# Moving the routing work of two expert layers: logits and turned rows tile by tile, modulation products behind them, places ahead of the rests

## The reference

```
g_prob = softmax(x @ w_group)            # 4 groups
g_sel  = argmax(g_prob + b_group)
e_prob = softmax((x @ w_expert) of the chosen group)   # 8 experts each
top-2 of e_prob + b_expert; weights normalized, times the group's probability
y[t] = sum over its 2 experts of weight * (silu(x @ w_gate[e]) * (x @ w_up[e])) @ w_down[e]
```

## Time and profile before

| | |
|---|---|
| median of three runs | 2175.79 us (2173.64 to 2178.47) |
| span of the profiled execution | 2172.9 us |
| PE busy | 2071.2 us, 95% |
| DVE, ACT busy | 1013.0 us, 718.1 us |
| mean granted TensorE clock | 0.979 |
| transfers | 621.14 MB, mean 286 GB/s |

### The profile page before, as it was taken

How to read it: one execution, slowest core, us unless ns; L and a number is a source line. 1 busy time by engine, 2 the same in 40 slices (tenths; PEclk the granted TensorE clock), 3 DMA queues, 4 the chain that set the end, 5 groups by cost and what they waited for, 6 DMA issues and landing times.

```text
span 2172.9 us, 31110 instructions
## 1 busy us (share of the span) xinstructions
PE 2071.2 (95%) x13436; PEld 1471.4 (68%) x13436; DVE 1013.0 (47%) x1665; ACT 718.1 (33%) x1074; POOL 214.5 (10%) x186
## 2 busy tenths in 40 slices
PE   5999999999999898999999998998999999999998
PEld 3855744444444696444444446987999989999998
DVE  3534511111111565111111115888579856777983
ACT  4334211111111442011111116867555444445552
POOL 0000000000000000000000000015135300003640
PEclk9999999999999999999999999999999999999999
DMA  9688799999999558999999995453455545334652
GB/s 330 211 299 321 289 411 423 422 423 422 423 423 422 213 205 331 415 423 422 423 422 423 423 423 195 156 194 118 152 159 182 187 177 132 102 117 156 193 176 97
DMA packets 220047, 621.14 MB, mean 286 GB/s; under 512 B 20544, under 2 KB 110464, under 8 KB 170496
## 3 DMA queue, kind: packets, MB, share of 16 engines
q1 hardware_dynamic: 209760, 612.80, 73.3%
q10 hardware_dynamic: 10144, 6.27, 1.0%
HBM read 617.95 MB, written 1.08 MB: 285 GB/s over the span
## 4 chain that ended last, share of the span: by engine, by line
PE 85%; DVE 6%; DMA 4%; ACT 3%; SPq 1%; issue 1%; POOL 0%; ACTq 0%; DVEq 0%
PE bank L593 31%; PE bank L1366 19%; PE bank L1375 10%; PE bank L1385 5%; PE bank L581 3%; PE bank L1345 3%; DMA ring<-in_moe_w_up 2%; PE bank L380 2%; PE bank L627 1%; PE bank L628 1%; DVE ring_rounded L309 1%; ACT ring_rounded L303 1%; DMA ring<-in_mla_w_dq 1%; PE bank L577 1%; PE bank L633 1%; SPq L280 1%
## 5 line engine op out<-in xcount | busy, mean ns | idle before, releaser
L593 PE MATMUL bank<-normed_rounded,ring_rounded 128*128 128x256 f32 x3424 | 416.0, 283 | 6.3 <-ACT normed_rounded L689 3.4
L593 PEld LDWEIGHTS bank<-normed_rounded,ring_rounded 128*128 128x128 f32 x3424 | 411.7, 189 | 8.3 <-issue 4.3
L1366 PE MATMUL bank<-ring,arena 128*64 128x512 f32 x1760 | 389.1, 592 | 3.1 <-DVE arena L1724 2.0
L1730 DVE TENSOR_TENSOR arena<-arena,bank 64x512 f32<-64x512 f32 x64 | 43.5, 680 | 648.1 <-ACT arena L1550 648.1
L309 DVE TENSOR_TENSOR ring_rounded<-ring,ring_rounded 128x4096 fp32r<-128x4096 f32 (+2 forms) x64 | 277.9, 4344 | 104.7 <-ACT ring_rounded L303 104.3
L593 PE MATMUL bank<-arena_rounded,ring_rounded 128*128 128x256 f32 (+1 forms) x2384 | 302.6, 286 | 4.5 <-ACT arena_rounded L1990 2.3
L1366 PEld LDWEIGHTS bank<-ring,arena 128*64 128x64 f32 x1760 | 127.2, 137 | 253.1 <-issue 250.0
L593 PEld LDWEIGHTS bank<-arena_rounded,ring_rounded 128*128 128x128 f32 x2384 | 290.7, 189 | 8.9 <-ACT arena_rounded L1990 3.1
L303 ACT ACTIVATE ring_rounded<-ring 128x4096 fp32r<-128x4096 f32 (+2 forms) x64 | 220.6, 3446 | 32.9 <-DMA ring<-in_ffn_w_down 31.7
L1375 PE MATMUL bank<-ring,arena 128*64 128x512 f32 x896 | 208.0, 607 | 3.8 <-ACT arena L1557 3.8
L1550 ACT ACTIVATE arena<-bank 64x512 f32<-64x512 f32 x64 | 38.1, 596 | 428.3 <-PE bank L1366 428.3
(11 more groups left out here) (286 smaller groups left out, 2154.1 us busy)
## 6 DMA issues: line engine op xcount, KB each, us to landing
ring<-in_moe_w_down SPq DMA_DIRECT2D x112, 1024.0 KB, 17.7
ring<-in_moe_w_gate SPq DMA_DIRECT2D x110, 1024.0 KB, 14.5
ring<-in_moe_w_up SPq DMA_DIRECT2D x110, 1024.0 KB, 16.2
ring<-in_w_mod SPq DMA_DIRECT2D x24, 2048.0 KB, 12.2
ring<-in_ffn_w_up SPq DMA_DIRECT2D x44, 1024.0 KB, 6.8
ring<-in_ssm_w_in SPq DMA_DIRECT2D x12, 2048.0 KB, 8.3
ring<-in_ffn_w_down SPq DMA_DIRECT2D x10, 2048.0 KB, 8.0
normed<-in_moe_w_gate SPq DMA_DIRECT2D x18, 1024.0 KB, 15.5
```

The lines of the kernel that those rows point to most:

```text
L593: end = e.matmul(out, lhs.bitcast(F32R), rhs.bitcast(F32R), start=start and n == 0 and k == 0, stop=stop and n == 2 and k == n_k - 1)
L1366: ends[i] = e.matmul(bank[rows, :], xt[:, n * KD // 2 + j, :], weights[:, j, :], start=n == 0 and j == 0, stop=n == 1 and j == KD // 2 - 1)
L1730: e.tensor_tensor(h, h, banks.of(key, "h", x)[0:cap, :], ALU.mult).then_inc(*dve.up(key, "h", x))
```

## The change

It reorders the routing of both layers. It leaves every product as it is.

- TensorE: the products with w_mod chunks 10 and 11 move from ahead of the logits to behind the turned rows. Logits and turned rows go by feature tile: for each i two logit products and two transposes. The four `row` banks are claimed ahead of these, the `acc` banks ahead of `ranks`.
- ScalarE: a first Exp of one column before the shift, so that the table is loaded there; `row high` of half 0 for both token tiles ahead of the Exp of the logits, half 1 behind it, then the modulation rows; then the eviction of `xt` parts 0 and 1, which VectorE did.
- VectorE: all four `lower` move behind `places_of(0)`, the modulation's reductions and the sum of loads; it evicts `xt` parts 2 and 3 in a row, then does weights, tables, shares 0 and 1 and `places_of(1)`; in the loop `turned_back(0)` comes behind `gated(0)`.

```diff
     def tensor(self, e, w):
-        for at in (10, 11):
-            self.last_steps.step_tensor(e, w, at, turn=False)
         k.meet(w, self.before)
...
-        for t in range(NT):
-            for i in range(KD):
-                w.wait_ge(*act.at(key, "x", i))
+        for half in range(2):
+            for t in range(NT):
+                _, emptied = banks.next(dve, key, "row", t, half)
+                w.wait_ge(*emptied)
+        for i in range(KD):
+            w.wait_ge(*act.at(key, "x", i))
+            for t in range(NT):
                 end = e.matmul(bank[:, t * n_log:(t + 1) * n_log], k.A[:, i, t * P:(t + 1) * P], self.W[:, i, :],
-                               start=i == 0, stop=i == KD - 1)
-        end.then_inc(*pe.up(key, "logits"))
-
-        for t in range(NT):
-            for half in range(2):
-                bank, emptied = banks.next(dve, key, "row", t, half)
-                w.wait_ge(*emptied)
-                for j in range(4):
-                    end = k.turn(e, bank[:, j * P:(j + 1) * P], k.A[:, 4 * half + j, t * P:(t + 1) * P])
-                end.then_inc(*pe.up(key, "row", t, half))
+                               start=i == 0 and t == 0, stop=i == KD - 1 and t == NT - 1)
+            if i == KD - 1:
+                end.then_inc(*pe.up(key, "logits"))
+            for t in range(NT):
+                at = i % 4 * P
+                end = k.turn(e, banks.of(key, "row", t, i // 4)[:, at:at + P], k.A[:, i, t * P:(t + 1) * P])
+                if i % 4 == 3:
+                    end.then_inc(*pe.up(key, "row", t, i // 4))
+        for at in (10, 11):
+            self.last_steps.step_tensor(e, w, at, turn=False)
         self.last_steps.turn_tensor(e, w, 10)
         self.last_steps.close_tensor(e, w)
...
-        first_rows, acc_emptied = [banks.next(dve, key, "xt", 0, 0)], []
...
+        first_rows = [banks.next(act if part < 2 else dve, key, "xt", 0, part) for part in range(KD // 2)]
...
-                w.wait_ge(*dve.at(key, "xt", x // TEAM, 2 * n + 1))
+                w.wait_ge(*(act if x < TEAM and n == 0 else dve).at(key, "xt", x // TEAM, 2 * n + 1))
...
     def scalar(self, e, w):
+        e.activation(k.root_of_one[:, 7:8], k.mat("ones")[:, 0:1], ACT.Exp).then_inc(*act.up())
...
+        row_high(0, 0)
+        row_high(1, 0)
+        w.wait_ge(*dve.at(key, "shifted"))
+        e.activation(self.prob, self.prob, ACT.Exp).then_inc(*act.up(key, "exp"))
+        row_high(0, 1)
+        row_high(1, 1)
         for at in (10, 11):
             self.last_steps.step_scalar(e, w, at)
...
+        for part in range(2):
+            w.wait_ge(*pe.at(key, "xt", 0, part))
+            e.activation(k_flat(self.xt[0][:, 2 * part:2 * part + 2, :]), banks.of(key, "xt", 0, part)[:, :], ACT.Copy
+                         ).then_inc(*act.up(key, "xt", 0, part))
...
     def vector(self, e, w):
-        lower(0, 0)
-        lower(0, 1)
         bank = banks.of(key, "ranks")
...
         places_of(0)
-        lower(1, 0)
-        lower(1, 1)
+        for at in (10, 11):
+            self.last_steps.step_vector(e, w, at)
         e.tensor_reduce(self.loads, ...)
+        for half in range(2):
+            for t in range(NT):
+                lower(t, half)
...
-        for part, between in enumerate((weights, shared, tables, lambda: self.last_steps.close_vector(e, w))):
-            turned_x(0, part)
-            between()
+        turned_x(0, 2)
+        turned_x(0, 3)
+        weights()
+        shared()
+        tables()
...
         shares(0)
+        shares(1)
+        places_of(1)
+        self.last_steps.close_vector(e, w)
...
-        shares(1)
-        turned_back(0)
-        places_of(1)
         for x in range(EXPERTS):
             gated(x)
+            if x == 0:
+                turned_back(0)
```

More of the change, by code:

```diff
@@ L1398, in tensor @@
         w.wait_ge(*self.router.at("router"))
-        for t in range(NT):
-            for i in range(KD):
-                w.wait_ge(*act.at(key, "x", i))
-                end = e.matmul(bank[:, t * n_log:(t + 1) * n_log], k.A[:, i, t * P:(t + 1) * P], self.W[:, i, :],
-                               start=i == 0, stop=i == KD - 1)
-        end.then_inc(*pe.up(key, "logits"))
-        for t in range(NT):
-            for half in range(2):
-                bank, emptied = banks.next(dve, key, "row", t, half)
-                w.wait_ge(*emptied)
-                for j in range(4):
-                    end = k.turn(e, bank[:, j * P:(j + 1) * P], k.A[:, 4 * half + j, t * P:(t + 1) * P])
-                end.then_inc(*pe.up(key, "row", t, half))
+        for half in range(2):
[5 more added lines that the diff above has]
+            for t in range(NT):
+                end = e.matmul(bank[:, t * n_log:(t + 1) * n_log], k.A[:, i, t * P:(t + 1) * P], self.W[:, i, :],
+                               start=i == 0 and t == 0, stop=i == KD - 1 and t == NT - 1)
[8 more added lines that the diff above has]
+            self.last_steps.step_tensor(e, w, at, turn=False)
         self.last_steps.turn_tensor(e, w, 10)
         self.last_steps.close_tensor(e, w)
+        acc_emptied = []
+        for b in range(KD // 2):
+            _, emptied = banks.next(dve, key, "acc", b)
+            banks.hold(key, "acc", b)
+            acc_emptied.append(emptied)
         bank, emptied = banks.next(dve, key, "ranks")
@@ L1535, in scalar, with row_high @@
                          ).then_inc(*act.up(key, "x", i))
+        def row_high(t, half):
+            w.wait_ge(*pe.at(key, "row", t, half))
+            e.activation(self.feats(self.f_high, t, half).bitcast(F32R), self.row_bank(t, half), ACT.Copy
+                         ).then_inc(*act.up(key, "row high", t, half))
+        row_high(0, 0)
[4 more added lines that the diff above has]
+        row_high(1, 1)
         for at in (10, 11):
             self.last_steps.step_scalar(e, w, at)
[L1538 to L1544, removed]
+        for part in range(2):
+            w.wait_ge(*pe.at(key, "xt", 0, part))
+            e.activation(k_flat(self.xt[0][:, 2 * part:2 * part + 2, :]), banks.of(key, "xt", 0, part)[:, :], ACT.Copy
+                         ).then_inc(*act.up(key, "xt", 0, part))
         def silu(x):
@@ L1730, in gated @@
             e.tensor_tensor(h, h, banks.of(key, "h", x)[0:cap, :], ALU.mult).then_inc(*dve.up(key, "h", x))
-        for at in (10, 11):
-            self.last_steps.step_vector(e, w, at)
-        for part, between in enumerate((weights, shared, tables, lambda: self.last_steps.close_vector(e, w))):
-            turned_x(0, part)
-            between()
+        turned_x(0, 2)
[3 more added lines that the diff above has]
+        tables()
         w.wait_ge(*dve.now())
         shares(0)
+        shares(1)
+        places_of(1)
+        self.last_steps.close_vector(e, w)
         reduced(self.most, self.loads, ALU.max)
```

## The result

The changed kernel is slower: median 2186.18 us against 2175.79 us, nine runs of each. The ratio on record for the runs is 1.0035, with a 95% interval of 1.0025 to 1.0045; the ratio of the two medians alone would be 1.0048. The forecast was 2189.5 with a range of 2177 to 2194. The profiled execution has a span of 2180.0 us, 7.1 above that of before.

The account below looks back on a forecast made before the run. TensorE and transfers were both full, the stream setting the loops' ends. Its added idle, +4.8 us in layer 0 and +8.9 in layer 1, gave +13.7: span 2172.9 to 2186.6, plus 2.9 for the median, 2189.5; range 2177 to 2194.

Parts of the forecast that it names:

- The mechanism: Both layers: late modulation products at clock 0.50 leave the full transfer stream standing; +4.8 us layer 0, +8.9 layer 1.
- the price of one feature tile at 0.50: Routing on TensorE: two logits and two turns for one i take 1.64 us at clock 0.50.
- fits ahead of 242.50: ScalarE before the first tile: early Exp with table load, 1.28 us, costed at nothing under a 2.42 us wait for VectorE.
- The first product: First modulation product behind the turned rows: starts at clock 0.50, takes 3.3 us, done at 259.3 in layer 0.
- The stream's sum: Transfers stand idle 11.6 us against 6.8 in layer 0, 11.4 against 2.5 in layer 1: +4.8 and +8.9 us.
- TensorE's own chain: Layer 0 routing at 0.50: gate_up +5.1 to +6.7 us, +2.4 to +5.7 after gains, so the stream decides.
- The small gains: TensorE around gate_up: 0.3 us (part 3), 0.7 (`gated(0)` ahead of others), up to 1.7 (slow down products) come back.
- The clock that never falls: Rival: TensorE stays at 1.00 through the routing; -1.6 us, 2174.2, no change that can be told; chance 0.10.
- the clock that comes back early: Rival: clock recovers during the mixture of logits and turns; +1.6 to +4.8 us, middle 2179.0; chance 0.18.
- The "faster" rival: Rival: clock holds and stream does not bind, so TensorE's chain alone counts; -8.2 us, 2167.6; chance 0.10.
- products are late and the stream does not bind: Rival: only TensorE's chain costs, twice +2.4 to +5.7 us, so +8, 2184; chance 0.05.
- The Trainium skill's rule: Routing mixture: by this rule the clock could not come back and 2189.5 stands; by the earlier trace it may, 2179.0.

Follow-up runs that it names:

- e1: Kernel before the change, with a quarter of the gate and up weights neither fetched nor used: 0.999 of the kernel before, median 2175.0 us.
- e2: Changed kernel with a quarter of the gate and up weights neither fetched nor used: 0.9976 of the kernel before, median 2172.33 us.
- e7: Kernel before with only the modulation products, and ScalarE's copies of their rows, moved behind the turned rows: 1.0034 of the kernel before, median 2183.78 us.
- e8: Changed kernel run again unaltered, on the chip of e5 to e7: 1.0037 of the kernel before, median 2185.77 us.
- e4: Changed kernel with modulation products back ahead of the logits, 32 filler products behind the turned rows, next bank set by hand: 0.9964 of the kernel before, 2168.24 us.
- e5: Changed kernel with modulation products back ahead of the logits and the next bank set by hand: 0.9962 of the kernel before, median 2168.85 us.
- e3: Changed kernel plus 32 filler products on constants ahead of the logits, modulation products still behind the turned rows: 0.9981 of the kernel before, median 2173.81 us.
- e6: Changed kernel with modulation products back ahead of the logits, interleaving undone, next bank set by hand: 0.9963 of the kernel before, median 2170.49 us.

## Why the prediction was right, and which terms were off

**The mechanism** stood as forecast. The stream binds both loops (e1 and e2 against the full kernels); the late products leave it standing (the holes in the routing of the changed kernel, e7 and e8, gone in e4 and e5), and that costs time (e3 against e4, and the loops of e5); TensorE's idle wait for the first tile takes the clock to 0.50 (e3 against the changed kernel), and the mixture does not bring it back; the second layer loses more than the first, because its stream had no hole before.

**The size** was too large: +13.7 us forecast, +9.4 by the traces, +10.4 by the medians, +7.6 by the ratio. The term that was mis-sized is the price of one feature tile at 0.50, put at 1.64 us (two logits at 0.61, two turns at 0.21) and measured at 1.17. The step that was wrong is "4.89 / 16 = 0.305 us each at clock 1.00". That quotient held waits for tiles. Two stretches of the kernel before show it:

```profile
243.20:245.90 2.70, 2.70 (x19) 1.00 1.01 425
246.00:248.00 2.00, 2.00 (x19) 1.00 1.02 426
```

(TensorE alone: length, busy time and instructions, clock, DMA share, GB/s.) While ScalarE still hands over tiles, 19 records take 2.7 us; behind the last tile 19 take 2.0, though the clock is the same and both are called busy. Unpaced, records start 0.11 us apart, and a logit product is two of them, 0.22 us; in e3 the mixture takes 5.0 us for eight tiles, 0.62 each, which leaves 0.20 for a logit beside a turn of 0.11. Doubled, 0.22 would have given 2 x 0.44 + 0.42 = 1.30 for a tile and, over eight tiles, 2.7 us less delay in each layer, 5.4 together, so +8.3.

**A term put at nothing** partly hid that. The forecast says that ScalarE's early Exp with its table load "fits ahead of 242.50". It did not. By program order it stands behind a wait that VectorE's reciprocal ends:

```profile
238.55 1.75 DVE L666 RECIPROCAL rstd<-rstd 128x256 f32<-128x256 f32 x1 [1.66 <-ACT rstd L661]
...
240.37 1.28 ACT L1534 ACT_TABLE_LOAD   x1 [1.85 <-DVE rstd L666]
241.66 0.20 ACT L1534 ACTIVATE root_of_one<-mats_rounded 128x1 f32<-128x1 f32 x1
241.77 3.29 ACT L1537 ACTIVATE normed<-normed,mod 128x256 f32<-128x256 f32 x8
```

ScalarE begins the first tile 4.05 and 4.06 us behind the sums (3.22 and 3.22 before the change, and in e7, which has no early Exp). So the first tile, the logits and the modulation products all come 0.8 us later in each layer, and the stream's standing time holds these 0.8 us too: an estimate of 1.7 us of the loss in both layers, which no run took out by itself. That the sum missed by only 4.3 us owes something to these two errors having opposite signs.

**The first product** took 255.6 - 252.1 = 3.5 us (forecast 3.3): the clock came back only at about 255.

**The stream's sum** worked with the delay put right. Read in stretches of 1 us, layer 0's queue ran dry at 248.1 (forecast 249.4; this execution's routing lies 1.6 us earlier) and bytes flow in earnest from 257.4, so 9.3 us idle against 6.8, +2.5; measured +2.6. Layer 1: dry at 846.1, flowing from 855.1, 9.0 against 2.5, +6.5; measured +6.8.

**TensorE's own chain** was forecast at +5.1 to +6.7 for gate_up and came at +1.6 and +1.2. Most of that is the same term (3.8 us for eight tiles). Part of the rest is the gather: it ran wholly at 1.00, 260.19 to 264.3 = 4.1 us, below the 5.2 that I had as its best (the 2.61 behind that figure lay partly at 0.50: the clock was 0.50 from 260.7 to 261.4). The small gains came fully, 2.4 us in each layer between the first and the second gate_up. That the rests come behind `mine` cost nothing, ScalarE's eviction took away gate_up's 0.97 us, and the first down products ran at 1.00 in both layers (3.65 us, against 5.35 in the earlier trace rows). All this is gain that the stream kept from showing, and that e5 and e6 show.

**The rivals.** The clock that never falls and the clock that comes back early did not happen; e3, with its filler, comes near to what the former would have been, 0.9981. The "faster" rival fell on both its conditions. That products are late and the stream does not bind is shown false by e1 and e2.

**The Trainium skill's rule** (TensorE: Matmul & The Clock Gate, Part 4: PE-mode transpose), that transposes do not count as work for the clock, stays undecided in this case. The changed kernel, e2 and e8 agree with it: nine us of logits and turned rows at 0.50 did not raise the clock. e7 tells little: its 3.3 us of turned rows alone passed at 0.50, and the clock rose within the dense products behind them. The earlier trace rows spoke against it, as the clock was 1.00 behind such a stretch. In e3, e4 and e5 the same mixture kept a clock of 1.00 for 5 us. The forecast's other reading, that logits alone do not hold the clock, is no rule either: in e6 all logits and then all turned rows ran at 1.00 (243.0 to 248.4 us), in the order of the kernel before, whose clock fell at the end of the logits. The measurements decide nothing general here but the two facts that the forecast needed: from 0.50 the mixture did not recover, and the clock rose only within the dense products behind it (whether these products or the time that had gone by raised it, no run tells).

**Not tried**: another order of SyncE's refills, so that the halves for `k.A` do not queue behind those for the w_mod slots; the banks' order by itself; and the changed kernel without the early Exp.

## What to carry to other kernels

Before moving work on a busy engine, list which slots its end frees and what is queued behind them: here 3.6 us of products, free while TensorE waited anyway, held six to eight halves of a stream that never had room to catch up. Where two resources are both full, count the standing time of the one that sets the end, from its queue's last byte to the next one that flows. Follow the other one's lateness past the first product of the loop: here it was made up by the second (e2), while in e7 it was not and came out in full at the end. And a part of a change can hide the gain of the rest: with that one move undone, the remaining parts give 0.38% (e5).

## What the runs showed of the hardware that was not expected

- A run of TensorE called busy over its whole length may still be paced by its producer: 19 records in 2.7 us while ScalarE made tiles, and in 2.0 us once it had ended, at the same clock of 1.00 and with 100% busy shown in both.
- The clock stayed where it was through the same mixture of 36-column products and transposes: at 1.00 where it began at 1.00 (e3, e4, e5, 5 us each), and at 0.50 where it began there (changed kernel, 9.4 us; e8, 9.5 us). Only these lengths were seen.
- Filler products cost nothing that can be told in these kernels: e4, with 3.6 us more of dense work for each layer, runs at 0.9964, e5 without it at 0.9962, and e4's gather ends earlier (gate_up 21.55 against 23.94 us behind the sums) by TensorE's clock alone.
